# Routing with fewer, wider steps, gathers issued in the routing block, and the first three expert pairs one by one

## The reference

```python
    group_p = jax.nn.softmax((flat @ rg_w + rg_b).astype(jnp.float32), axis=-1)      # 4 groups
    g_idx = jnp.argmax(group_p, axis=-1)
    p_group = jnp.max(group_p, axis=-1, keepdims=True)
    e_logits = (flat @ re_w + re_b).astype(jnp.float32).reshape(n, N_GROUPS, EXPERTS_PER_GROUP)
    e_p = jax.nn.softmax(e_logits[jnp.arange(n), g_idx], axis=-1)
    top_p, top_i = lax.top_k(e_p, TOP_K)                                             # 2 of the group's 8
    top_p = top_p / jnp.sum(top_p, axis=-1, keepdims=True)
    ...
    for e in range(N_EXPERTS):                                                       # 32 experts, 1024 x 256
        h = jax.nn.silu(flat @ w_gate[e]) * (flat @ w_up[e])
        y = y + gates[:, e:e + 1] * (h @ w_down[e])
```

## Time and profile before

| | |
|---|---|
| median of 3 runs | 1660.35 us (1652.09 to 1667.23) |
| profiled execution | 1651.96 us, of which the span is 1649.8 us |
| mean granted TensorE clock | 0.923 |
| DMA over the whole span | 285.62 MB, mean 173 GB/s |
| PE / DVE / ACT / POOL busy | 83% / 40% / 35% / 14% of the span |

### The profile page before, as it was taken

The page is one execution under the profiler, slowest core; times in us unless marked ns, Lnnn a source line. Parts: engine busy times, 40 slices in busy tenths (PEclk is TensorE's granted clock), DMA queues, the critical chain, the costliest instruction groups (busy, mean ns, idle before and its releaser), DMA issues. The chain is left out here.

```text
span 1649.8 us, 37746 instructions
## 1 busy us (share of the span) xinstructions
PE 1364.2 (83%) x16476; PEld 826.6 (50%) x16476; DVE 652.3 (40%) x1003; ACT 583.5 (35%) x879; POOL 234.8 (14%) x191
## 2 busy tenths in 40 slices
PE   5799999991898898999996879999999538787780
PEld 3455545551788888888885334344434413222220
DVE  1437677765444444444442360343413331000004
ACT  4225554543565555555552561000002102111113
POOL 0011111221321333333330000000000001000002
PEclk9999999996899999999998989999999659889896
DMA  8205445534432233322203209734455446999984
GB/s 350 83 10 170 128 134 154 162 94 125 99 93 71 77 78 81 84 80 80 80 24 138 105 1 392 278 128 177 146 197 227 185 185 274 427 425 424 424 358 178
DMA packets 169321, 285.62 MB, mean 173 GB/s; under 512 B 43331, under 2 KB 141763, under 8 KB 155091
## 3 DMA queue, kind: packets, MB, share of 16 engines
q1 hardware_dynamic: 163220, 254.00, 43.6%
q0 software_dynamic: 5952, 29.36, 4.6%
HBM read 236.14 MB, written 55.59 MB: 177 GB/s over the span
## 5 line engine op out<-in xcount | busy, mean ns | idle before, releaser
L390 PE MATMUL pr_ps<-hT,pr_w 128*128 128x512 f32 x384 | 170.5, 601 | 15.3 <-ACT pr_rate L451 10.7
L941 DVE COPY_PREDICATED rc_T<-masks_sb,rc_ps 128x512 f32<-128x512 uint32 x96 | 65.3, 731 | 159.2 <-PE rc_ps L737 159.2
L390 PEld LDWEIGHTS pr_ps<-hT,pr_w 128*128 128x128 f32 x384 | 73.1, 192 | 108.2 <-issue 87.9
L1208 PE MATMUL mg_ps<-hT,mg_w 128*128 128x512 f32 x256 | 111.2, 593 | 1.0 <-PEq L1102 1.0
L703 PE MATMUL rc_ps<-rc_KR,rc_BK 64*128 64x128 f32 (+1 forms) x768 | 55.8, 292 | 37.1 <-DMA rc_KR<-kr_chunks 36.2
L737 PE MATMUL rc_ps<-rc_T,rc_Z 64*64 64x64 f32 x3840 | 75.2, 223 | 11.8 <-issue 10.3
L1665 DVE TENSOR_TENSOR mg_w<-mg_w,ex_pgu 128x256 f32<-128x256 f32 x16 | 6.7, 421 | 196.9 <-ACT mg_w L1659 196.9
L1208 PEld LDWEIGHTS mg_ps<-hT,mg_w 128*128 128x128 f32 x256 | 48.6, 190 | 62.5 <-issue 62.5
L863 ACT ACTIVATE rc_Z<-rc_ps 128x1024 f32<-128x1024 f32 (+1 forms) x48 | 41.4, 881 | 104.4 <-PE rc_ps L703 104.4
L881 ACT ACTIVATE rc_G<-rc_ps 128x512 f32<-128x512 f32 x120 | 66.3, 599 | 28.9 <-PE rc_ps L737 28.5
L1227 ACT ACTIVATE mg_sig<-mg_ps 128x512 f32<-128x512 f32 x16 | 9.6, 597 | 183.8 <-PE mg_ps L1208 183.8
(11 more groups left out here) (328 smaller groups left out, 2689.4 us busy)
## 6 DMA issues: line engine op xcount, KB each, us to landing
bonus_sb<-in_ada_w SPq DMA_DIRECT2D x16, 1024.0 KB, 7.0
ex_top<-in_w_experts SPq DMA_DIRECT2D x8, 2048.0 KB, 17.4
mg_w<-in_w_merge SPq DMA_DIRECT2D x8, 1792.0 KB, 7.7
pr_w<-in_w_prep SPq DMA_DIRECT2D x8, 1664.0 KB, 6.6
kr_chunks<-pr_KR SPq DMA_DIRECT2D x16, 768.0 KB, 4.8
bk_chunks<-pr_BK SPq DMA_DIRECT2D x16, 768.0 KB, 6.8
rc_BK<-bk_chunks SPq DMA_DIRECT2D x24, 512.0 KB, 5.4
rc_KR<-kr_chunks SPq DMA_DIRECT2D x24, 512.0 KB, 5.4
```

What stands on the lines that cost most here:

```text
L390: last = pe.matmul(lat_bank[:, :], wv[:, j * KT + kt, :], hT[:, kt, lat], start=(kt == 0), stop=(kt == KT - 1))
L941: dve.copy_predicated(T[u][:, d, :, :, :].rearrange("p q b t -> p b q t"), level(int(s[1:]), d), by_side).then_inc(dve_s, 1)
L1208: last = pe.matmul(ps[u][j][:, :], w[:, u, w0 + k, :], rhs, start=(k == 0), stop=(k == n - 1))
```

## The change

In `route`, the products of the counts become five wider ones: one gives `rt_totals` (from `both` of all four tiles, 128 columns), and has its own semaphore step; four give the prefix counts. VectorE sums the totals over tiles. VectorE's steps are regrouped, so that steps that don't need each other stand together ahead of one drain, and loops over groups or tiles become single wider instructions. POOL waits for `tok` within the block and issues the gathers of pairs 0 and 1 there. ScalarE has one `Sigmoid` of a single column at the block's end. `first_row` and `row_n` move into the space of masks that are no longer used.

In `experts`, SP waits for both of these gathers before it loads expert 6. TensorE and ScalarE do pairs 0, 1 and 2 one by one: `down(p)` stands right behind `turn_hidden(p)`. From pair 3 on the order is the old one.

```diff
+def gather_tokens(pool, g, rows, list_):
+    return pool.indirect_dma_start(out=rows, out_offset=None, in_=g["f_dram"], in_offset=bass.IndirectOffsetOnAxis(ap=list_, axis=0))
...
                 pool.drain().then_inc(cst, 1)
+                pool.wait_ge(tok_s, 1)
+                for p in range(2):
+                    gather_tokens(pool, g, xe[:, p, :], R["tok"][:, p:p + 1]).then_inc(g["gathered"][p], 16)
...
+                act.activation(warm[:, :], g["small"][:, 1:2], ACT.Sigmoid)
...
-                for t in range(NT + 1):
-                    for q in range(t):
-                        last = pe.matmul(ps[:, t, :], g["mask"]("ones"), both[:, q, :], start=(q == 0), stop=(t == NT and q == t - 1))
-                    if t < NT:
-                        last = pe.matmul(ps[:, t, :], g["mask"]("before"), both[:, t, :], start=(t == 0), stop=True)
+                every = lambda x, t0, t1: x[:, t0:t1, :].rearrange("p t e -> p (t e)")
+                pe.matmul(every(totals, 0, NT), g["mask"]("ones"), every(both, 0, NT), start=True, stop=True).then_inc(pref, 1)
+
+                pe.matmul(every(ps, 0, NT), g["mask"]("before"), every(both, 0, NT), start=True, stop=False)
+                for t in range(1, NT):
+                    last = pe.matmul(every(ps, t, NT), g["mask"]("ones"), every(both, 0, NT - t), start=False, stop=(t == NT - 1))
...
-                for q in range(4):
-                    src = el[:, :, 8 * q:8 * q + 8]
-                    if q == 0:
-                        tt(sel[:, :, :], src, gh[:, :, 0:1].to_broadcast([P, NT, 8]), ALU.mult)
-                    else:
-                        tt(te[:, :, :], src, gh[:, :, q:q + 1].to_broadcast([P, NT, 8]), ALU.mult)
-                        tt(sel[:, :, :], sel[:, :, :], te[:, :, :], ALU.add)
+                tt(prod, el.rearrange("p t (q e) -> p t q e", q=NG), gh[:, :, :].unsqueeze(3).to_broadcast([P, NT, NG, EPG]), ALU.mult)
+                red(sel[:, :, :], prod.rearrange("p t q e -> p t e q"), ALU.add)
...
-                tt(both[:, :, :], O1[:, :, :], O2[:, :, :], ALU.add)
-                dve.drain().then_inc(both_ready, 1)
+                dve.tensor_tensor(both[:, :, :], by_token(chosen[:, 0, :]), by_token(chosen[:, 1, :]), ALU.add).then_inc(both_ready, 1)
...
-                cnt = ps[:, NT, :]
+                red(cnt[:, :].unsqueeze(2), totals[:, :, :].rearrange("p t e -> p e t"), ALU.add)
...
-                ts(over[:, :], tmpc[:, :], 0.0, None, ALU.is_gt)
-                for j in range(1, SEQ // P):
-                    dve.scalar_tensor_tensor(out=over[:, :], in0=tmpc[:, :], scalar=float(j * P), in1=over[:, :], op0=ALU.is_gt, op1=ALU.add)
-                    dve.drain()
+                tt(above4[:, :, :], above[:, :].unsqueeze(2).to_broadcast([P, NE, NT]), first_row[:, 0:NT].unsqueeze(1).to_broadcast([P, NE, NT]), ALU.is_gt)
+                red(over[:, :].unsqueeze(2), above4[:, :, :], ALU.add)
...
-                dve.tensor_copy(R["tok"][:, :], pt[:, :])
+                dve.tensor_copy(R["tok"][:, :], pt[:, :]).then_inc(tok_s, 1)
...
                     if n >= WSLOTS:
                         sp.wait_ge(s["down"], (n - WSLOTS) // 2 + 1)
+                    else:
+
+                        for v in range(2):
+                            sp.wait_ge(g["gathered"][v], 16)
...
                 turn_tokens(0)
-                gate_up(0)
-                turn_tokens(1)
-                turn_hidden(0)
-                for p in range(PAIRS):
+                for p in range(FIXED // 2):
+                    gate_up(p)
+                    turn_tokens(p + 1)
+                    turn_hidden(p)
+                    down(p)
+                gate_up(FIXED // 2)
+                turn_tokens(FIXED // 2 + 1)
+                turn_hidden(FIXED // 2)
+                for p in range(FIXED // 2, PAIRS):
```

More of the change, by code:

```diff
@@ L1547, in _ @@
-                tt(base[:, FIXED:NE], base[:, FIXED:NE], tmpc[:, FIXED:NE], ALU.add)
-                tt(tmpc[:, :], cnt, cap[:, :], ALU.subtract)
-                ts(over[:, :], tmpc[:, :], 0.0, None, ALU.is_gt)
-                for j in range(1, SEQ // P):
-                    dve.scalar_tensor_tensor(out=over[:, :], in0=tmpc[:, :], scalar=float(j * P), in1=over[:, :], op0=ALU.is_gt, op1=ALU.add)
-                    dve.drain()
+                dve.tensor_scalar(down[:, :], rank[:, :], float(-P), float(last), ALU.mult, ALU.add)
@@ new lines, in _ @@
+                dve.tensor_scalar(up[:, :], rank[:, :], float(2 * P), float(FIXED // 2 * P - last), ALU.mult, ALU.add)
+                dve.tensor_scalar(cap[:, FIXED:NE], rank[:, :], float(HALF), float(2 * BIG - P), ALU.is_lt, ALU.mult)
+                dve.drain()
+                dve.scalar_tensor_tensor(out=up[:, :], in0=rank[:, :], scalar=float(HALF), in1=up[:, :], op0=ALU.is_lt, op1=ALU.mult)
+                dve.tensor_scalar(cap[:, FIXED:NE], cap[:, FIXED:NE], float(P - BIG), None, ALU.add)
@@ new lines, in _ @@
+                dve.drain()
+                dve.tensor_tensor(base[:, FIXED:NE], down[:, :], up[:, :], ALU.add)
+                dve.tensor_tensor(above[:, :], cnt[:, :], cap[:, :], ALU.subtract)
+                dve.drain()
+                tt(above4[:, :, :], above[:, :].unsqueeze(2).to_broadcast([P, NE, NT]), first_row[:, 0:NT].unsqueeze(1).to_broadcast([P, NE, NT]), ALU.is_gt)
+                red(over[:, :].unsqueeze(2), above4[:, :, :], ALU.add)
+                dve.tensor_tensor(away[:, :], base[:, :], cap[:, :], ALU.add)
@@ L1562, in _ @@
[L1562 to L1567, removed]
@@ L1568, in _ @@
-                dve.drain()
-                for j, o in enumerate((O1, O2)):
-                    dve.tensor_reduce(slot[:, j, :].unsqueeze(2), o[:, :, :], X, ALU.add)
+                dve.wait_ge(pref, 2)
+                dve.tensor_tensor(above[:, :], incl[:, :], over[:, :], ALU.subtract)
+                dve.tensor_tensor(tmp[:, :, :], ps[:, :, :], cap[:, :].unsqueeze(1).to_broadcast([P, NT, NE]), ALU.is_ge)
+                dve.tensor_tensor(pos[:, :, :], ps[:, :, :], base[:, :].unsqueeze(1).to_broadcast([P, NT, NE]), ALU.add)
@@ new lines, in _ @@
+                dve.drain()
+                dve.tensor_scalar(above[:, :], above[:, :], float(PAIRS), float(P), ALU.add, ALU.mult)
+                dve.drain()
+                tt(away[:, :], above[:, :], away[:, :], ALU.subtract)
+                tt(tmp[:, :, :], tmp[:, :, :], away[:, :].unsqueeze(1).to_broadcast([P, NT, NE]), ALU.mult)
+                tt(pos[:, :, :], pos[:, :, :], tmp[:, :, :], ALU.add)
+                place = chosen.rearrange("p j (t e) -> p (j t) e", e=NE)
+                for j in range(2):
+                    dve.tensor_tensor(by_token(chosen[:, j, :]), by_token(chosen[:, j, :]), pos[:, :, :], ALU.mult)
@@ L1571, in _ @@
                 dve.drain()
+                red(slot[:, :, :].rearrange("p j t -> p (j t)").unsqueeze(2), place, ALU.add)
                 flat_slot = slot[:, :, :].rearrange("p j t -> p (j t)")
@@ L1602, in load_expert, with experts @@
     sp.dma_start(dn, src[:, n:EXPERT_W]).then_inc(sem_, 16)
-def experts(nc, g, I, R, ew, wl, small, out):
+def experts(nc, g, I, R, ew, wl, xe, small, out):
     NT = SEQ // P
@@ L1742, in fetch @@
                 def fetch(p):
[L1743 to L1748, removed]
+                    pool.wait_ge(s["turned"], p - 1)
+                    gather_tokens(pool, g, xe[:, p % 2, :], R["tok"][:, p:p + 1]).then_inc(g["gathered"][p % 2], 16)
+                fetch(2)
                 def keep(p):
@@ L1767, in body @@
                     pool.sem_inc(g["noted"]["pool"], 1)
-                    gather(pool, 0, idx[:, 0, 0:1]).then_inc(gathered, 16)
+                    gather_tokens(pool, g, xe[:, 0, :], idx[:, 0, 0:1]).then_inc(gathered, 16)
                 spill(pool, body)
@@ L1847, in sig, with rows @@
                     sigmoid(act, p % 2).then_inc(s["sig"], 1)
-                xt(0)
-                sig(0)
-                xt(1)
-                for p in range(PAIRS):
+                def rows(p):
+                    act.wait_ge(s["down"], p + 1)
+                    if p >= 2:
+                        act.wait_ge(yst[p % 2], p // 2 * 16)
+                    copy_y(act, y[:, p % 2, :]).then_inc(s["y"], 1)
+                xt(0)
+                for p in range(FIXED // 2 + 1):
+                    sig(p)
+                    xt(p + 1)
+                    if p < FIXED // 2:
+                        rows(p)
+                for p in range(FIXED // 2, PAIRS):
                     if p + 1 < PAIRS:
@@ L2055, in program @@
                  "spill_expert": msb("spill_expert", [P, SPILL], I32), "spill_tiles": msb("spill_tiles", [P, 1], I32)}
-            route(nc, g, I, logits, R, ew, wl)
             g["gathered"] = [mixers.enter_context(nc.semaphore(f"ex_gathered{v}")) for v in range(2)]
-            experts(nc, g, I, R, ew, wl, small, out)
+            xe = line(g["hT"])[:, 0:2 * D].rearrange("p (v n) -> p v n", v=2)
```

(2 more changed lines are left out.)

42 lines of the change are left out of this document (16 added, 26 removed).

## The result

The changed kernel takes 1634.26 us in the median of 4 runs (1632.43 to 1638.13) against 1659.18 of 4 runs before; the ratio is 0.9851, 95% interval 0.9802 to 0.9901. In a later comparison on one chip, with 6 runs of it, it was 1630.79 against 1652.73 of 10 runs, ratio 0.9876 (0.9849 to 0.9904); an eleventh run before, a slow one of 7654.55 us, is left out. The profiled execution took 1635.48 us, span 1633.5.

The account below looks back on a forecast made before the run. The prediction took the full DMA queue, started by the load of expert 7, to bound the pairs' stage. Its terms 8.5 + 2.7 + 4.3 + 7.7 = 23.2 us, off the median 1660.35, gave 1637, range 1625 to 1651.

Parts of the forecast that it names:

- the landing: First gather's issue to TensorE's start on the first pair: 6.0 us in place of 10.3, so -4.3 us.
- What bounds the stage: Pairs' stage, 217 us: lasts as long as its bytes take, counted from the load of expert 7.
- Rival (a): Pairs' stage: the new order of pairs brings nothing, only routing and gathers count; -15.5 us, 1645; chance 0.08.
- Routing: Routing block up to `tok`: TensorE's counts no longer awaited (-5.0), fewer and regrouped VectorE steps; -8.5 us in sum.
- The earlier issue: First gather's issue: POOL issues it 0.3 us after `tok` in place of 3.0, so -2.7 us.
- Rival (d): Routing block: POOL's wait opens late or VectorE holds it; -21 us, 1639; chance 0.80 together with the main case.
- in the block POOL waits for `tok` alone: Routing block: the ground for taking 0.3 us from `tok` to POOL's first gather.
- the tail of experts 3 to 5: First gather: overlap with the last transfer of these experts' loads, landed by 1329 at the latest, costs up to 1 us.
- Rival (b): First gather: slow by itself, not through expert 6's traffic, taking 10.3 us again; -18.9 us, 1641.5; chance 0.09.
- One by one: Pairs 0 to 2: `down(0)` ends earlier, so the load of expert 7 comes at 1366.9 in place of 1374.63, -7.7 us.
- the cover of 17.1 us: First pairs: the queue needs 17.1 us per pair of experts, which hides TensorE's 13.2 us per pair with its waits.
- Rival (c): Pairs 0 to 2: shorter pieces with waits keep TensorE at 1.2 GHz, the queue runs dry; +24 us, 1684; chance 0.03.

Follow-up runs that it names:

- all pairs one by one: The changed kernel with each down(p) right behind its own turn_hidden(p) for all 16 pairs, against the kernel before: 0.9846, 1629.06 us.
- light loads: Changed kernel, loads of experts 7 to 31 cut to half of gate and up, an eighth of down: new pair order 1575.78 us, old order 1571.62.
- the order alone: The kernel before with only the new order of pairs 0 to 2: 0.9953 of the kernel before, 7.7 us in the medians.
- the gathers alone: The kernel before with only POOL's wait and two gathers in the routing block and SP's wait for them: 0.9979, 4.9 us in the medians.

## Why the prediction was right

It gave 1637 with a range of 1625 to 1651; measured were 1634.26, and a gain of 24.9 us (21.9 in the later comparison) for 23.2. That the sum hit so closely is in part luck: the clock's rise and its fall near the end move a run by up to 3 us, and the landing was forecast 1.4 too high. The prediction also gave 0.77 to a gain that stands clear of 1%; with an interval that ends at 0.9901, the first comparison doesn't quite show that much.

**What bounds the stage** was right and carried the rest. The stretch under full DMA has 217 us in the earlier trace rows, in the trace after and with all pairs one by one; light loads turn the order's gain into a loss. The stage's length shows it most sharply: in the ten traces with full loads whose later pairs keep the old order, `gate_up(15)` starts 221.3 to 221.7 us behind the load of expert 7, whenever that load comes. Rival (a) is out by the order alone.

**Routing**, 8.5 forecast (its own terms add up to 8.4), 8.2 measured. The wait went whole; the steps by levels took 0.3 more.

**The earlier issue** was 2.7 in both. The rule of the Trainium skill (SBUF — State Buffer, "SBUF: two separate sides") would have let VectorE's last two microseconds hold the gather back. The trace shows no such hold: the gather started 0.29 behind `tok`, beside them. No row tells whether these steps ran in a two-port mode. The issue took 1.29 us in place of the 1.04 in the earlier trace rows, and 0.25 us is the most that this rule, if it is the cause, is worth there. Rival (d) is out.

**The landing** is the mis-sized term: 4.3 forecast, 2.9 measured. The gather itself was faster than the 6.0 that I took. The step that failed is "in the block POOL waits for `tok` alone", as if nobody waited for POOL: the block's end does, until its transfers have landed, so that the first pair starts with the second gather. I had put up to 1 us down to the tail of experts 3 to 5, which in the trace after landed at about 1335.1, beside the first gather; the gathers alone, with that tail long over, start the first pair 7.18 us behind the issue, and the kernels with it 7.14 to 7.50. Rival (b) is out, since the first gather lands in 5.2 us.

**One by one**, 7.7 forecast, 7.6 from before to after, 7.7 in the medians of the order alone (6.8 in its trace, where the clock rose 1.9 us later). A pair took 12.9 us for the 13.2 forecast, so the cover of 17.1 us held even with the clock late. Rival (c) didn't come: the clock rose, though between 5.8 and 8.8 us into the first pair, which moves the load of expert 7 by up to 1.6 us.

**The last 1.3 us**, from the load of expert 7 to the end, were forecast at nothing and aren't a gain of the change. They are mostly `gate_up(15)`, 1.7 us shorter at the higher clock. Other traces with the order of three pairs have 272.7 to 276.7 us in this stretch, and that instruction group 7.1 to 10.0.

## What to carry to other kernels

Where a stage lives on a full queue, look for what issues its first transfer: each microsecond there came off the end, whether it was won in routing, in a gather or in TensorE's order, and TensorE's own overlap was worth nothing as long as a pair stayed under the 17.1 us of its weights. Test that with lighter transfers before relying on it, because the same order then costs 4 us. And an indirect gather moved ahead of a block's end brings its landing into that end: move the one that is wanted first, and no more. That gave 2.2 us at the first pair's start; at the end it is shown only together with all pairs one by one.

## What the runs showed of the hardware

TensorE's first instruction behind the block's end came 0.3 to 0.5 us behind the landing of POOL's last transfer, with one gather (5.2 us behind its issue), with two (7.1 to 7.5 behind the first) and with 2 MB more (12.9), while POOL's last instruction was over 4 to 10 us earlier. The one exception has TensorE's transposes in the block: there ScalarE's copy of them ended last, and TensorE went on 0.5 behind it. Which instruction of the end does the waiting wasn't tried.

TensorE's clock, granted at 0.50 in all traces when the first pair began, rose between 5.8 and 8.8 us into it, with the same work from there in all but the one that has the transposes in the block. With it the load of expert 7 came between 18.4 and 20.0 us behind the pair's start, in the new order. What sets the moment wasn't tried.

Near the end, TensorE waited for the last weights ahead of `gate_up(15)`. In seven of the twelve traces with full loads it waited 1.2 to 2.2 us, the clock was granted at 1.00 behind that, and `gate_up(15)` took 7.1 us; in the other five it waited 2.3 to 4.1 us, and with a mean clock of 0.70 to 0.83 it took 8.5 to 10.0.
